# Five of the eight input tiles of the output projection computed in fp32 inside attention

## The reference

```python
p = softmax(s)                    # scores of queries and keys, with the forget sums
hc = p @ v                        # group C
mix = concatenate([ha, hb, hc]) @ w_out[l]
x = x + g1 * mix
```

## Time and profile before

| what | value |
|---|---|
| median of three runs | 2899.29 us |
| span of the profiled execution | 2905.2 us |
| time of the profiled execution beside its span | the page gives none of its own; its span lies within the three runs |
| TensorE busy | 2763.6 us (95%) |
| VectorE busy | 1186.2 us (41%) |
| ScalarE busy | 659.8 us (23%) |
| GpSimd busy | 424.7 us (15%) |
| attention, layer 0 and layer 1 | 400 to 625 us, 1832 to 2049.5 us |
| output projection, layer 0 | 624 to about 724 us |

### The profile page before, as it was taken

One profiled execution on the slowest core, in us unless ns is written; L12 is line 12 of the kernel. 1 busy time (PEld: TensorE's weight loads), 2 busy tenths in 40 slices (PEclk: granted clock), 3 DMA queues, 4 the chain that ended last, 5 costly groups with the idle time before them and its releaser, 6 DMA issues. The chain is left out here.

```text
span 2905.2 us, 48336 instructions
## 1 busy us (share of the span) xinstructions
PE 2763.6 (95%) x20492; PEld 2553.9 (88%) x20492; DVE 1186.2 (41%) x2069; ACT 659.8 (23%) x1122; POOL 424.7 (15%) x424
## 2 busy tenths in 40 slices
PE   5999988889999999999999999878999999999998
PEld 3999965569999999999989999545899999999998
DVE  5625524346532422424355344333564233242344
ACT  4334323333111111001133432333231001001011
POOL 1101114340000000001111000244300001001010
PEclk9999989899999999999999999899999999999999
DMA  7440157741222222111224101776302111111111
GB/s 299 146 105 30 64 193 272 252 148 44 66 88 84 81 84 73 59 44 44 66 106 117 48 30 66 267 262 223 125 31 86 54 49 44 44 59 44 44 58 68
DMA packets 106873, 295.36 MB, mean 102 GB/s; under 512 B 19606, under 2 KB 32791, under 8 KB 104611
## 3 DMA queue, kind: packets, MB, share of 16 engines
q1 hardware_dynamic: 106498, 291.49, 29.8%
q0 software_dynamic: 160, 0.79, 0.1%
HBM read 269.61 MB, written 22.63 MB: 101 GB/s over the span
## 5 line engine op out<-in xcount | busy, mean ns | idle before, releaser
L304 PE MATMUL PS<-hH,whi 128*128 128x352 f32 x1632 | 533.2, 327 | 8.0 <-DVE hL L2193 6.4
L304 PE MATMUL PS<-hL,whi 128*128 128x352 f32 x1632 | 523.8, 321 | 0.0
L304 PE MATMUL PS<-hH,wlo 128*128 128x352 f32 x1632 | 523.4, 321 | 0.0
L304 PE MATMUL PS<-aH,whi 128*128 128x352 f32 x1344 | 439.6, 327 | 9.2 <-DVE aL L251 9.1
L304 PE MATMUL PS<-aL,whi 128*128 128x352 f32 x1344 | 432.7, 322 | 0.0
L304 PE MATMUL PS<-aH,wlo 128*128 128x352 f32 x1344 | 432.4, 322 | 0.0
L292 POOL CAST whi<-raw 128x1024 fp32r<-128x1024 f32 x158 | 167.6, 1061 | 1672.6 <-PE PS L304 1336.5
L304 PEld LDWEIGHTS PS<-hH,whi 128*128 128x128 f32 x1632 | 306.7, 188 | 16.7 <-issue 11.8
L304 PEld LDWEIGHTS PS<-hL,whi 128*128 128x128 f32 x1632 | 307.4, 188 | 0.0
L304 PEld LDWEIGHTS PS<-hH,wlo 128*128 128x128 f32 x1632 | 306.4, 188 | 0.0
L824 PE MATMUL PS<-aH,whi 128*128 128x352 f32 x912 | 303.7, 333 | 1.9 <-ACT F L1022 1.9
(11 more groups left out here) (353 smaller groups left out, 3840.8 us busy)
## 6 DMA issues: line engine op xcount, KB each, us to landing
KVp<-kv SPq DMA_DIRECT2D x256, 384.0 KB, 4.3
raw<-w_ff SPq DMA_DIRECT2D x128, 512.0 KB, 3.5
raw<-w_in SPq DMA_DIRECT2D x42, 512.0 KB, 3.5
wad_single<-w_ada SPq DMA_DIRECT2D x40, 512.0 KB, 3.5
wad<-w_ada SPq DMA_DIRECT2D x32, 512.0 KB, 5.5
x_spill<-x SPq DMA_DIRECT2D x2, 4224.0 KB, 13.9
wada<-w_first SPq DMA_DIRECT2D x8, 1024.0 KB, 7.2
raw<-w_out SPq DMA_DIRECT2D x16, 512.0 KB, 4.3
```

Source lines behind the costliest of these rows:

```text
L304: last = nc.tensor.matmul(PS[:, 3 * p + part, 0:CW], w[:, k, :], a[:, k, part * CW:(part + 1) * CW], start=k == 0 and w is wh and a is hig ...
```

## The change

- In attention, eight panels of w_out are loaded with their first five k tiles (READY = 5: the rows of groups A and B, which are ready when attention starts), 327 KB each, and multiplied in plain fp32 with F[:, MIX[k]]: 24 pieces of 5 matmuls each (new part_product(c)). Two pieces follow query_key(i) in each even iteration; they use PSUM banks 1 and 3, which an even unit leaves free. ScalarE copies each piece out. Panels 0 and 1 stay in SBUF (rows of keys that are no longer needed); the pieces of the other six are stored to DRAM (mix_parts) by DMAs that ScalarE issues, 18 of 176 KB.
- The ring of pages has 20 buffers, RING = 5; the room goes to the weights and the rows to be stored.
- The probabilities are no longer multiplied by GpSimd. VectorE takes the reciprocal widened to 128 columns, TensorE transposes it beside the result, ScalarE copies it (inverse_out), and VectorE multiplies the result with it (mixed).
- In the output projection only k = 5, 6, 7 are split, loaded and multiplied. The stored parts and x come back in pairs of panels (load_pair). GpSimd adds the stored part to ev (join_part) before VectorE's residual, for the wide and the narrow phase, and its splits of weights stand between these adds.

```diff
+                if i in (2, 4, 9, 13, 17, 21, 25):
+                    part_weights((2, 4, 9, 13, 17, 21, 25).index(i) + 1)
...
-    kv0 = [small0 + 3072 * i for i in early + tuple(i for i in range(22) if i not in early)] + [aH0 + 3072 * i for i in range(2)]
+    kv0 = [small0 + 3072 * i for i in early + tuple(i for i in range(2, 22) if i not in early)]
...
-                        nc.gpsimd.tensor_scalar(Trow[i % 2][e][:, 0:n], Trow[i % 2][e][:, 0:n], sums[:, i % 4, e:e + 1], None, ALU.mult)\
-                            .then_inc(S["scaled"], 1)
...
+                    if qb >= 4:
+                        pe.wait_ge(S["part_out"], i + 1)
...
-                        pe.wait_ge(S["scaled"], 2 * u + e + 1)
+                        pe.wait_ge(S["exp"], 2 * u + e + 1)
...
+                    pe.wait_ge(S["inverted"], u + 1)
+                    nc.tensor.transpose(PS[:, bank[key], P:2 * P], inverse[u % 2][:].rearrange("p e d -> p (e d)"), ident)
...
+                def part_product(c):
+                    p, part = divmod(c, NCH)
+                    pe.wait_ge(part_loaded, 16 * (p + 1))
+                    for k in range(READY):
+                        last = nc.tensor.matmul(PS[:, 1 + 2 * (c % 2), 0:CW], wpart[p % 3][:, k, :], F[:, MIX[k], part * CW:(part + 1) * CW],
+                                                start=k == 0, stop=k == READY - 1)
+                    last.then_inc(S["part_done"], 1)
...
                         query_key(i)
+                        if i % 2 == 0:
+                            part_product(i)
+                            part_product(i + 1)
...
+                def mixed(u):
+                    j, qb = units[u]
+                    key = ("mixed", u)
+                    is_full(dve, key)
+                    dve.wait_ge(S["inverse_out"], u + 1)
+                    nc.vector.tensor_tensor(F[:, QC + j, qb * P:(qb + 1) * P], PS[:, bank[key], 0:P], norms[u % 2][:], ALU.mult).then_inc(S["dve"], 1)
...
-                        nc.vector.reciprocal(sums[:, i % 4, :], sums[:, i % 4, :]).then_inc(S["shares"], 1)
+                        wide = sums[:, i % 4, :].rearrange("p (e o) -> p e o", o=1).to_broadcast([P, 2, DH])
+                        nc.vector.reciprocal(inverse[i % 2][:], wide).then_inc(S["inverted"], 1)
...
+                def part_store(c):
+                    p, at_ = PANELS[c // NCH], c % NCH * CW
+                    if p not in DIRECT:
+                        act.wait_ge(S["part_out"], c + 1)
+                        act.dma_start(mix_parts[:, p, at_:at_ + CW], part_row[c % 2][:]).then_inc(part_stored[c % 2], 16)
...
                         exps(i)
+                        if i % 2 == 0:
+                            part_out(i)
...
+                    if i < NU and i % 2 == 0:
+                        part_out(i + 1)
+                        part_store(i)
...
-                load_x(0)
+                def load_pair(i):
+                    if i >= 2:
+                        sp.wait_ge(pair_loaded[i % 2], landed_pair(i - 2))
+                    sp.dma_start(x[:, 2 * i:2 * i + 2, :], x_spill[:, 2 * i:2 * i + 2, :]).then_inc(pair_loaded[i % 2], 16)
+                    if i:
+                        for j in (2 * i, 2 * i + 1):
+                            sp.dma_start(mix_part[j][:], mix_parts[:, j, :]).then_inc(pair_loaded[i % 2], 16)
+                load_pair(0)
                 for n in range(2, AHEAD):
                     load(sp, n)
+                    if n < KT // 2 + 1:
+                        load_pair(n - 1)
...
+                def join_part(ph, j):
+                    pool.wait_ge(s["room"], (2 * (j + 1), 2 * KT + j + 1)[ph])
+                    if j >= 2 and ph == 0:
+                        pool.wait_ge(pair_loaded[j // 2 % 2], landed_pair(j // 2))
+                    t = ev[j % 2][:, COLS[ph]]
+                    nc.gpsimd.tensor_tensor(t, t, mix_part[j][:, COLS[ph]], ALU.add).then_inc(joined, 1)
...
-                for n in range(4, KT):
-                    split_high(pool, n)
-                for n in range(KT, AHEAD):
+                for j in range(KT):
+                    join_part(0, j)
+                    if j < 4:
+                        split_high(pool, 4 + j)
+                for j in range(KT):
+                    join_part(1, j)
+                    if j < 2:
+                        split_high(pool, KT + j)
+                for n in range(KT + 2, AHEAD):
                     split_high(pool, n)
```

More of the change, by code:

```diff
@@ L285, in load @@
                 sp.wait_ge(s["split"], before + 1)
-            sp.dma_start(raw[spot(n)][:], source(n).rearrange("a p k n -> (a p) k n")).then_inc(loaded[spot(n)], 16)
+            sp.dma_start(raw[spot(n)][:, tiles(n)], source(n).rearrange("a p k n -> (a p) k n")[:, tiles(n)]).then_inc(loaded[spot(n)], 16)
         def split_high(pool, n):
@@ L291, in split_high @@
                 pool.wait_ge(s["done"], freed(n))
-            nc.gpsimd.tensor_copy(home(n)[0][:], raw[spot(n)][:]).then_inc(s["high"], 1)
+            nc.gpsimd.tensor_copy(home(n)[0][:, tiles(n)], raw[spot(n)][:, tiles(n)]).then_inc(s["high"], 1)
         def split_low(dve, n):
@@ L296, in split_low, with part_product @@
             dve.wait_ge(s["high"], n + 1)
-            nc.vector.tensor_tensor(wl[:], raw[spot(n)][:], wh[:].bitcast(F32), ALU.subtract).then_inc(s["split"], 1)
+            nc.vector.tensor_tensor(wl[:, tiles(n)], raw[spot(n)][:, tiles(n)], wh[:, tiles(n)].bitcast(F32), ALU.subtract).then_inc(s["split"], 1)
         return s, load, split_high, split_low
-    def part_product(p, part, k, high, low, home=None):
+    def part_product(p, part, k, high, low, home=None, first=0):
         wh, wl = home or (whi[p], wlo[p])
@@ L304, in part_product @@
             last = nc.tensor.matmul(PS[:, 3 * p + part, 0:CW], w[:, k, :], a[:, k, part * CW:(part + 1) * CW],
-                                    start=k == 0 and w is wh and a is high, stop=k == KT - 1 and w is wl)
+                                    start=k == first and w is wh and a is high, stop=k == KT - 1 and w is wl)
         return last
@@ L1408, in trunk @@
     RING = len(kv0) // GP
+    READY = 5
+    wpart = [tile(f"wpart{i}", [P, READY, P], a) for i, a in enumerate((aH0, aH0 + 2560, small0 + 3072))]
+    part_row = [tile(f"part_row{i}", [P, CW], small0 + 4 * CW * i) for i in range(2)]
+    DIRECT = {0: KC, 1: KC + 1}
+    mix_rows = [16, 17, 8, 9, 10, 11, 12, 18]
+    mix_part = [tile(f"mix_part{j}", [P, TOK], row_at(r)) for j, r in enumerate(mix_rows)]
+    PANELS = (2, 3, 4, 0, 5, 6, 1, 7)
+    NPART = KT * NCH
     D0 = aH0 + 2 * 3072
@@ L1430, in trunk @@
     future = tile("future", [P, P], T0 + 256, BF16)
+    inverse = [tile(f"inverse{i}", [P, 2, DH], T0 + 512 + 512 * i) for i in range(2)]
+    norms = [tile(f"norms{i}", [P, P], T0 + 1536 + 512 * i) for i in range(2)]
     units = [(j, qb) for j in range(PAIRS) for qb in (0, 7, 2, 5, 1, 6, 3, 4)]
@@ L1484, in attention @@
     def attention(l):
-        names = ("filled", "act", "dve", "qk", "low", "exp", "shares", "scaled", "chain", "zero", "query", "cumulated", "fill", "min", "past_exp", "pad",
-                 "past_mixed", "gap", "share", "weights", "selected", "masks")
+        names = ("filled", "act", "dve", "qk", "low", "exp", "inverted", "inverse_out", "chain", "zero", "query", "cumulated", "fill", "min", "past_exp", "pad",
+                 "past_mixed", "gap", "share", "weights", "selected", "part_done", "part_out")
         S = {n: sem(f"fox_{n}") for n in names}
@@ L1492, in attention @@
         kvl = [sem(f"fox_kv{i}") for i in range(RING)]
+        part_loaded = sem("fox_part_loaded")
+        part_stored = [sem(f"fox_part_stored{i}") for i in range(2)]
         hp = lambda e: slice(64 * e, 64 * e + 64)
@@ L1504, in has_room @@
                 is_empty(pe, slots[index[key] - 4][0])
+        stored_before = lambda c: sum(PANELS[m // NCH] not in DIRECT for m in range(c % 2, min(c, NPART), 2))
         with nc.Block() as block:
@@ L1907, in _ @@
                         nc.scalar.activation(share[:], share[:], ACT.Exp).then_inc(S["share"], 1)
+                for i in range(2):
+                    act.wait_ge(part_stored[i], 16 * stored_before(NPART + i))
     def out_and_mlp(l):
@@ L1971, in _ @@
                     load(sp, n)
[L1972 to L1976, removed]
+                    if n < KT // 2 + 1:
+                        load_pair(n - 1)
+                    if n == KT and not last_layer:
+                        sp.dma_start(nxt[:], next_params[l]).then_inc(nxt_loaded, 16)
                     if n == KT:
@@ L2022, in third @@
                 def third(n, part, operands, tile_ready=None, half=None):
-                    for k in range(KT):
+                    first_k = READY if n < KT else 0
+                    for k in range(first_k, KT):
                         if tile_ready:
                             tile_ready(k)
```

(10 more changed lines are left out.)

95 lines of the change are left out of this document (59 added, 36 removed).

## The result

The changed kernel takes 3069.38 us (median of 4 runs, 3065.78 to 3076.83), the kernel before 2900.44 in the same comparison: a ratio of 1.0579, 95% interval 1.0559 to 1.0599. The direction was forecast, the size was not: 2956 was expected, and 3069 lies outside the range.

What follows compares the result with a forecast made beforehand. Attention was taken as bound by a loop of page ring and tensor work, the projection by TensorE, then GpSimd's joins. Per layer +40 - 11.5 = +28.5; two give +57, so 2899 + 57 = 2956 us, range 2915 to 3000.

Steps and rivals of the forecast that it cites:

- the price of an fp32 product: Attention pieces: 0.315 us a product, 120 a layer, 38 us of tensor work added against 57 lost in the projection.
- S: Batch loop from finished scores to the next past products: forecast 2.3 us longer a period, including 3.15 for pieces.
- Rival E: Attention pieces: fp32 takes four passes, +38 us a layer, 3032 us; chance 2%.
- The ring: Attention page buffers: 20 instead of 24 leave four more pages to land before the scores, +3.6 us a period.
- D: Batch loop from the start of past products to finished scores: forecast 15.5 to 19.7 us, counted as +3.6.
- The late division: Attention: GpSimd's scaling leaves the path, minus 1.0 us a period; transposed reciprocals add 0.15.
- the tail: Attention after the last past products: loses 2 us a layer of GpSimd waits.
- The start of attention: Beginning of attention: adds 4 us a layer, from two weight loads within the first 16 pages and 2.3 again.
- The output projection: Wide phase: joins bound it, sums of squares begin near 58 us instead of 69.7; gain 11.5 us a layer.
- a turn of it: Output projection's closed loop of join, residual, sum of squares, split_low, load, split_high, join: 8.4 us.
- The narrow phase: Output projection's later phase: gains nothing, bounds minus 2 to plus 4 us, as VectorE's work stays.
- Rival D, the clock: TensorE pauses at scores and in the wide phase, then runs at 1.2 GHz: +20 us a layer, 2996 us; chance 11%.

Runs made afterwards that it cites:

- the experiment: Kernel before with each of the 12 fp32 pooling products issued five times, 48 products more: 2923.63 us, ratio 1.0085.
- The experiment: Kernel before with only the edits that take the reciprocals off GpSimd, 24 page buffers and no pieces: 2906.05 us, ratio 1.0022.
- the ring alone: Kernel before with the page buffers cut from 24 to 20 and nothing else: 2973.53 us, ratio 1.0246.
- the pieces at the scores: Changed kernel with three pieces just ahead of each batch's scores instead of two behind each even query_key: 2986.84 us, ratio 1.0287.

## Why the prediction was wrong

- **The step that failed: the price of an fp32 product.** "six of them take 2.04 us ... I take 0.315". The six records at L845 are three products: its loop issues three for one j. A product is two records, 0.59 to 0.61 us by the experiment, and its records follow each other 0.30 us apart at a granted clock of 1.00. The whole argument for the change hangs on this: 120 x 0.48 = 57 us of split products leave a layer and 120 x 0.59 = 71 us of fp32 products enter it (82 us as they ran, part of them at the lower clock), so tensor work rises by at least 13 us where I had it fall by 19. In S it made 5.9 us a period instead of 3.15: 14 x 2.7 = 38 us of the 113 us missing.
- **Rival E was the right rival with 2%.** The Trainium skill (FP8 and Floating Point Precision, TensorE Precision Notes) says that a true fp32 product makes 4 passes. By the rows of the runs a product takes 0.59 to 0.61 us; four times 0.159 is 0.64. In its time the trace agrees with the page to within 8%; the passes themselves do not show, only two records. What spoke against the page was my count. Counting the records of a line against the products that its code issues would have settled it: x24 for 12.
- **The ring: right in mechanism, undersized.** Forecast +3.6 a period for D, measured +4.3 alone and +4.8 in the changed kernel. I had taken 0.6 off for batches late by PE's own work; once the pages are later than that work, nothing is off. With the 0.8 in S, where I had nothing, the ring is 74 us by itself instead of 50.
- **The late division: no gain.** I subtracted 1.0 a period for GpSimd's waits, 2 a layer for the tail and 3 for PT, 24 us in two layers, and added 2 for the transposes. The experiment shows plus 6 us for all of it. That is some 28 us of error: a wait that goes was taken as time that goes. The changed kernel fits: its S of 15.8 us is the ring's 9.9 and the 5.9 of a pair of pieces at the full clock.
- **The start of attention.** From its first load to the first past products 28.5 us became 34.9, 6.4 a layer against 4. With the ring alone it was 28.0, so this is not the ring.
- **The output projection: right in mechanism, and the number in part by luck.** Sums at 58.3 us against 58, and the ring is there. But a turn of it took 6.6 to 7.3 us against 8.4 (its terms add up to 8.5), since the join takes 1.66 and not 2.0 and the load about 2.5 and not 2.9; and the joins of panels 6 and 7 began only 51 and 54 us into the block, after waits for ScalarE's ev (7.92 and 1.15 us). The two errors cancel. The narrow phase, forecast to gain nothing, lost 3.9 us. The join's 1.66 us agree with the estimate of 1.6 us worked out from the Trainium skill (GPSIMD Engine Reference, Elementwise — side-by-side cycle accounting).
- **The sum from the trace.** Period +11.5 x 14 = 161, starts +13, ends -1, output projection -15: 158 of the 160 by which the spans differ. Held against the forecast, the errors are 38 us for the pieces in S, 24 for the ring, 28 for the division, 8 for the output projection, 5 for the starts and 7 for the 0.5 us by which D exceeds that of the ring alone: 110 of the 113 us missing. The ring and the division are taken from times of runs, the others from traces, so that the sum closes this well is not a proof of each term.
- **The range.** Its own bounds, +60 a layer for attention and nothing for the projection, give 2899 + 120 = 3019, not 3000. Its lower bound for attention, +15, is 40 less the 25 us of seven times 3.6; with most of the page waits gone too, as it says, it would be near +3. The measured time lies above either upper end.

Rival D, the clock, finds no support in the changed kernel: from first to last past products it had 0.89, the kernel before 0.90. Beyond that the clock's part is not separated. With the pieces at the scores it rose to 0.98 beside a gain of twice the expected size; with the ring alone it fell to 0.84, but there four pages at 1.04 us are 4.2 of the 5.1 us a period without it.

## What to carry to other kernels

Count the records of an operation against what its line of code issues before you take a duration from them; a product may be more than one record. Work that is moved into an idle stretch must go to the place of the wait: the same pieces cost their full length two iterations away and almost nothing just ahead of the instruction that waits. A ring of buffers whose consumer and next producer are one short stretch apart has no slack, and each buffer taken from it cost a transfer in every period here (4.3 us for four).

## What the runs showed of the hardware

A plain fp32 product of 128 x 128 weights with 352 columns is two matmul records that follow each other in 0.30 us at a granted clock of 1.00, 0.59 to 0.61 us in all, more than three fp32r products of the same shape (0.48). GpSimd's add of 704 columns took 1.66 us. Where it ran beside an operation of VectorE on 704 columns (0.95 us by itself), one of the two took longer in the changed kernel: 2.33 us for VectorE's residual at 751.82, 2.16 for GpSimd's add at 764.19.
